# Scaling the prompt attention's exponentials on GpSimd instead of VectorE

## What is computed

```
s = einsum('nbqhd,nbkhd->nbhqk', qb, kk) * HEAD_DIM ** -0.5      # block of 128 queries, 256 keys (previous and own block)
logits = where(valid, s + bias, NEG_INF)
lse = logsumexp(logits, axis=-1)
p = exp(logits - lse)                                            # each row divided by its sum
o = einsum('nbhqk,nbkhd->nbqhd', p, vv)
alpha = softmax(stack(lses, axis=2), axis=2)                     # weights of the three branches
out = (o * alpha).reshape(N, T, ATT_WIDTH) @ w_o
```

## Time and profile before

| | us |
|---|---|
| median of three runs | 2800.95 |
| lowest and highest run | 2794.38, 2804.59 |
| profiled execution, its own time | 2803.53 |
| its span | 2801.7 |
| TensorE busy | 2593.8 (93%) |
| VectorE busy | 1311.9 (47%) |
| ScalarE busy | 974.2 (35%) |
| GpSimd busy | 940.0 (34%) |

### The profile page before, as it was taken

How to read it: one execution, slowest core, us unless ns; L and a number is a source line. 1 busy time by engine, 2 the same in 40 slices (tenths; PEclk the granted TensorE clock), 3 DMA queues, 4 the chain that set the end, 5 groups by cost and what they waited for, 6 DMA issues and landing times.

```text
span 2801.7 us, 40988 instructions
## 1 busy us (share of the span) xinstructions
PE 2593.8 (93%) x16414; PEld 2459.6 (88%) x16414; DVE 1311.9 (47%) x1515; ACT 974.2 (35%) x2208; POOL 940.0 (34%) x489
## 2 busy tenths in 40 slices
PE   5899989999999999999898988938999999999996
PEld 3777769999999999999898986738999999999996
DVE  3678865554344444444711205685643333333335
ACT  3311214443333343433611303422533333333333
POOL 1322215253344444443341300043444343434330
PEclk7999989999999999999899957768999999999997
DMA  7476540043333444422022162200111111111101
GB/s 266 153 217 198 165 142 31 8 150 142 107 136 140 154 154 154 154 76 76 16 98 65 58 231 76 84 31 16 52 53 46 46 46 42 46 44 46 45 31 68
DMA packets 90315, 270.55 MB, mean 97 GB/s; under 512 B 27584, under 2 KB 37504, under 8 KB 88352
## 3 DMA queue, kind: packets, MB, share of 16 engines
q1 hardware_dynamic: 90144, 267.96, 28.1%
HBM read 236.12 MB, written 58.67 MB: 105 GB/s over the span
## 4 chain that ended last, share of the span: by engine, by line
PE 78%; DVE 8%; issue 5%; DMA 4%; ACT 2%; SPq 2%; POOL 1%; POOLq 0%; DVEq 0%; ACTq 0%
PE bank L263 48%; PE bank L1512 17%; PE bank L282 3%; DMA w_raw<-in_ws 1%; PE bank L1580 1%; PE bank L1725 1%; PE bank L1662 1%; DMA w_raw<-in_att 1%; PE bank L305 1%; PE bank L381 1%; POOL w_lo L249 1%; PE bank L368 1%; SPq L653 1%; PE bank L1540 1%; PE bank L1606 1%
## 5 line engine op out<-in xcount | busy, mean ns | idle before, releaser
L263 PE MATMUL bank<-h_hi,w_hi 128*128 128x352 f32 x2832 | 617.6, 326 | 16.0 <-issue 9.7
L263 PE MATMUL bank<-h_hi,w_lo 128*128 128x352 f32 x2832 | 612.2, 324 | 0.0
L263 PE MATMUL bank<-h_lo,w_hi 128*128 128x352 f32 x2832 | 611.4, 324 | 0.0
L249 POOL TENSOR_TENSOR w_lo<-w_raw,w_hi 128x1024 fp32r<-128x1024 f32 x182 | 483.9, 2660 | 133.5 <-ACT w_hi L1056 120.1
L263 PEld LDWEIGHTS bank<-h_hi,w_hi 128*128 128x128 f32 x2832 | 481.4, 189 | 38.8 <-issue 27.6
L1159 DVE SCALAR_TENSOR_TENSOR cv<-u,cwb,cv 128x1072 f32<-128x1072 f32 x88 | 154.1, 1751 | 758.7 <-ACT cv L916 758.7
L263 PEld LDWEIGHTS bank<-h_hi,w_lo 128*128 128x128 f32 x2832 | 488.0, 188 | 0.0
L263 PEld LDWEIGHTS bank<-h_lo,w_hi 128*128 128x128 f32 x2832 | 482.1, 188 | 0.0
L245 POOL CAST w_hi<-w_raw 128x1024 fp32r<-128x1024 f32 x168 | 204.6, 1218 | 604.1 <-DMA w_raw<-in_ws 327.6
L476 ACT ACTIVATE tb<-bank,mod 128x352 f32<-128x352 f32 x552 | 261.0, 544 | 254.8 <-PE bank L1512 173.0
L787 POOL TENSOR_TENSOR z_lo<-cv,z_hi 128x1024 fp32r<-128x1024 f32 x44 | 110.4, 2508 | 472.8 <-ACT z_hi L934 472.8
(11 more groups left out here) (239 smaller groups left out, 2862.9 us busy)
## 6 DMA issues: line engine op xcount, KB each, us to landing
w_raw<-in_ws SPq DMA_DIRECT2D x182, 512.0 KB, 5.4
w_mod<-in_wm SPq DMA_DIRECT2D x72, 512.0 KB, 5.9
out_kvs<-in_cache SPq DMA_DIRECT2D x8, 4088.0 KB, 19.8
w_modf<-in_wm SPq DMA_DIRECT2D x40, 512.0 KB, 4.2
w_raw<-in_att SPq DMA_DIRECT2D x36, 512.0 KB, 3.5
shifts<-full SPq DMA_DIRECT2D x128, 129.5 KB, 2.4
x<-in_xt SPq DMA_DIRECT2D x8, 1056.0 KB, 10.7
out_kvs<-in_cache SPq DMA_DIRECT2D x8, 1016.0 KB, 9.2
```

What stands on the lines that cost most here:

```text
L249: e.tensor_tensor(w_lo[s][:, :], w_raw[s][:, :], w_hi[s][:, :].bitcast(F), ALU.subtract).then_inc(split[s], 1)
L263: mm = e.matmul(bank[3 * b + c][:, 0:CW], w[s][:, kk * P:(kk + 1) * P], a[:, kk, c * CW:(c + 1) * CW], start=(kk == 0 and q == 0), stop=(k ...
```

## The change

`normalise` moves from VectorE's list to GpSimd's. It is the same four instructions a step, on the same tiles, behind the same semaphores: it waits for `rs` (the inverse sums) and raises `norm` (for which TensorE's turn waits). VectorE's list goes from the inverse sums of n + 1 straight to the logits of n + 2. On GpSimd all 24 steps stand ahead of the first split of the output weights, with `weigh(0)` between the scalings of steps 20 and 21.

```diff
@@ gpsimd
+            def normalise(n):
+                u, q = n // 4, n % 4
+                e.wait_ge(at_["rs"], n + 1)
+                for hp in range(2):
+                    for i in range(2):
+                        b = 2 * q + i
+                        lo = 0 if PREV[u % 3][b] else P
+                        last = e.tensor_scalar(lg[n % 4][:, hp, i, lo:256], lg[n % 4][:, hp, i, lo:256],
+                                               rsum[:, u, hp, b:b + 1], None, ALU.mult)
+                last.then_inc(at_["norm"], 1)
...
-            weigh(0)
+            for n in range(NQ):
+                normalise(n)
+                if n == 20:
+                    weigh(0)
             e.wait_ge(at_["o_ready"], 3)
             for s in range(4):
                 put(e, "wo", s, 0)
@@ vector
             inverse_sums(0)
-            normalise(0)
...
                 if n + 1 < NQ:
                     inverse_sums(n + 1)
-                    normalise(n + 1)
                 if n + 2 < NQ:
                     logits(n + 2)
```

More of the change, by code:

```diff
@@ L1214, in logits @@
                                 ALU.mult).then_inc(at_["nm"], 1)
[L1216 to L1225, removed]
             def inverse_sums(n):
```

## The result

The changed kernel takes 2808.84 us (median of 20 runs, 2805.15 to 2815.81) where the kernel before, in the runs beside it, takes 2804.32 us (20 runs, 2794.38 to 2811.12). The ratio is 1.0017 with a 95% interval of 1.0009 to 1.0024, so 2.5 to 6.7 us are lost. That lies inside the 0.5% called no change and inside the range, but on the other side of zero than the forecast of some 5 us less.

The account below looks back on a forecast made before the run. TensorE was taken to bound the prompt attention early and VectorE late. Early steps 0, middle 0 and tail -4.7 us took the profiled 2803.53 us to 2798.8, given as 2796 because that execution lay above the median; range 2788 to 2814.

Parts of the forecast that it names:

- What GpSimd pays: Price of one scaling on GpSimd, estimated two thirds up between bounds: 0.35 us narrow (128 columns), 0.58 wide (256).
- One tensor input speaks for the cast: Argument for pricing GpSimd's scaling toward the one-input cast's rate, the lower bound: 0.13 us narrow, 0.26 wide.
- Early steps: Steps 0 to 5: TensorE's work hides a 4.4 us loop; net zero, from -0.8 to +0.9 us.
- Rival 1: GpSimd's scaling is slow: at twice the upper bound, early steps lengthen and the total is +28 us, 2829; chance 0.13.
- rival 3's opposite: From 1702 to 1730 us TensorE's granted clock falls from 0.90 to 0.61, adding 11.9 us, giving 2808; chance 0.03.
- The gain that I set against the slip: Early steps: 0.81 us leave the chain as logits stop queuing behind a scaling, against first turns 0.7 us late.
- The hold on flips: VectorE's sign flip of the maxima can wait for one GpSimd instruction, up to 0.58 us; 0.2 taken early.
- Middle: Steps 6 to 18: TensorE sets the pace to 1774 us, so nothing counted, zero.
- Tail: Steps 18 to 23: VectorE is the bound and loses the scalings; -4.7 us, from -6.9 to -2.9.
- sample rows: Tail: their VectorE subtraction falls from 2.49 to 0.42 us because GpSimd's output-weight splits come later; -2.1 us.
- first maximum: Second half's first maximum on VectorE comes earlier and meets GpSimd's last output-weight split; +1.6 us.
- the alternation: Step 21: VectorE's three products with 1/z alternate with GpSimd's scalings, giving about 0.5 of 0.78 us back; net -0.25.

Follow-up runs that it names:

- the cut ones: Changed kernel with each scaling cut to 24 of 128 or 120 of 256 columns, the rest left unscaled: 2802.32 us, 0.9983 of the kernel before.
- the head alone: Kernel before with only the scalings of steps 0 to 17 on GpSimd, output-weight splits where they stood: 2814.06 us against 2806.78, ratio 1.0030.
- the tail alone: Kernel before with only the scalings of steps 18 to 23 on GpSimd, output-weight splits behind them: 2804.41 us, ratio 0.9990.

## Why the prediction was wrong

**What GpSimd pays: the step that failed.** A scaling took 0.60 us narrow and 0.91 wide, where I took 0.35 and 0.58 and set an upper bound of 0.46 and 0.74. With the cut ones, 0.343 us for 24 columns (the median) and 0.565 for 120 (a quarter of 2.26), and 0.602 for 128 columns (the shortest single one) and 0.907 for 256 (a quarter of 3.63), the price is about 0.3 us plus 2.4 ns a column (0.36, 0.59, 0.61 and 0.91 by that line). A column costs a little more than in the two-input subtraction, 2.17 ns, and the fixed part is more than its 0.19. "One tensor input speaks for the cast" was wrong: per column the scaling is as dear as an instruction with two tensors. That the scalar of each partition makes it so is not shown; no run multiplied by a constant on GpSimd. The bound failed because the line through the two subtractions was taken for the dearest that the engine can be, and no row said so. The Trainium skill, GPSIMD Engine Reference, section 4.1, holds one-input work to be roughly at line rate, 0.38 us for 256 columns by the estimate from section 3.1 in the prediction; the 0.91 measured here does not bear this out for a scaling with a scalar per partition, while its rule, elementwise work on VectorE, does hold here: 0.35 us there. (By the forecast's own bounds, 3.0 us between 0.26 and 0.58, a price of 0.38 would have made the sum nearly 2 us better, not 1.)

**Early steps: zero became +8.** Rival 1's formula gives the loop with the measured price: 1.09 + 0.68 + 0.18 + 0.1 + 3.63 = 5.7 us, and 5.67 were found; steps 0 to 3 lost 3.0 us by it. Rival 1 was the right mechanism, at 1.2 to 1.3 times the upper bound, about where it was said to outweigh the tail. The other 4.9 us, in steps 3 to 6, are rival 3's opposite, a fall of the granted clock, which I put beside the forecast as a case of its own at 0.03. The runs show that it hangs on rival 1: a loop that makes TensorE wait takes its clock with it, though not by the same amount each time (steps 3 to 6 lost 4.9 and 5.1 us in the changed kernel's two traces, 1.5 with the head alone). The two should have been one case, with a price nearer 8 us than 3. The gain that I set against the slip was also too small: with the short scalings steps 3 to 6 take 21.64 us against 23.5, so 1.9 where I counted 0.81, since both scalings on that chain leave it.

**The hold on flips: right, small.** The flip of the maxima (L1227 now) takes 170 ns at least, 190 in the median and 482 at most: 0.31 us of hold in the worst step where I took 0.2, and next to none in most. The added row ahead of GpSimd's first scaling took 11 ns, as forecast.

**Middle: zero, as far as can be seen.** In steps 12 to 15, at a clock of 0.71, TensorE's own work covers even four wide scalings of 3.63 us: 23.38 us with them on either engine. Whatever the scalings cost elsewhere is lost in the scatter of the middle, 74.1 to 85.9 us among kernels that scale on VectorE.

**Tail: right in sign and in its largest item, 2 us too good.** From the starts of VectorE's instructions in the first trace of each, item by item in us:

| from, to | forecast | measured |
|---|---|---|
| turn 18 to copy of 19 (step 19) | -0.35 | +0.1 |
| to the first branch sum (step 20) | -0.6 | -0.9 |
| to the copy of 21 (step 21) | -0.25 | +1.0 |
| to the low parts (step 22) | -0.6 | 0.0 |
| to the copy of 22 (sample rows) | -2.1 | -2.4 |
| to the last turn (step 23) | -2.35 | -1.45 |
| sum | -6.25 | -3.7 |
| first maximum | +1.6 | +1.0 (+0.2 in the second traces) |

The sample rows came about as forecast, the return at the maximum was smaller. Steps 21 and 23 are the price again. In step 21 there is a second error: I had VectorE's products pay for the alternation, and GpSimd paid. The three products take 3.58 us against 3.49 in before, while the scaling beside them takes 4.92 instead of 2.34. In step 22 the logits of step 23 then wait 0.77 us for scores that stand on TensorE's list behind the late turn 21. With the upper price I had the tail at -2.9; the tail alone measured -2.4.

**The sum.** At the forecast's own price -4.7 was forecast and -4.5 measured, in part by luck, as told above. At the real price the head's +8 to +9, the tail's -3.3 to -3.7 and the maximum's +0.2 to +1 make about +5, against +4.5.

## What to carry to other kernels

Before an instruction moves to an engine on which no row prices it, measure it there: the whole sign hung on 0.9 against 0.58 us. A new wait on TensorE has to be priced with the clock that may go with it; here 3 us of waiting took another 5 in two traces, and 1.5 in a third. When a change does two things (here the scalings' engine and the splits' place), try each alone: the gain was in the second, and the best kernel, 8 us under the one before, has it with only those three scalings moved that other waits covered.

## What was not expected of the hardware

- GpSimd's multiplication by a scalar per partition: about 0.3 us plus 2.4 ns a column of 128 partitions, 0.91 us for 256 columns, 2.6 times VectorE's 0.35. Why it costs so much stays open.
- Beside three two-input products of VectorE, back to back, it was GpSimd that waited: four scalings took 4.92 us instead of 2.34 while the products took 3.58 instead of 3.49. It isn't always so: beside GpSimd's two-input subtractions VectorE's first maximum took 2.24 us instead of 1.20.
- One wait of TensorE of 1.42 us, at the end of a step in which the granted clock was 1.00, was followed by a step at 0.52; with matmuls in its place that step ran at 1.00 (one trace of each).
- In two traces of one kernel the granted clock from turn 12 to 15 was 1.00 and 0.75, and the stretch took 17.07 and 22.03 us, though their times differ by 2 us (2803.53 and 2805.52): a stretch's gain read from one trace can be the clock's. Here most of it was given back elsewhere: from the first turn to the last the second trace is 8 us longer, over the whole only 2.
